# Block 2's RMS norms: token scale taken out of the matmul operand and put into the evictions

## The reference, cut to what matters

```python
def rms_norm_2(x, g):
    y = x * rsqrt(mean(x*x, -1) + EPS)
    return y * g
h = h + hybrid_mixer(rms_norm_2(h, attn_norm_g), w_in, forget_b, ret_norm_g, w_out)   # retention + forgetting attention
h = h + conv_ffn(rms_norm_2(h, ffn_norm_g), w_up, conv_w, conv_b, w_down)             # silu(conv(a)) * b
return rms_norm_2(h, final_norm_g)
```

## Time and profile before

| | |
|---|---|
| median of three runs | 2331.92 us |
| profiled execution, its own time | 2332.22 us |
| its span (first to last instruction) | 2330.3 us |
| granted TensorE clock, mean | 0.994 |
| PE busy | 2264.8 us (97%) |
| DVE / ACT / POOL busy | 908.9 / 886.6 / 1206.2 us |

### The profile page before, as it was taken

The page is one execution under the profiler, slowest core; times in us unless marked ns, Lnnn a source line. Parts: engine busy times, 40 slices in busy tenths (PEclk is TensorE's granted clock), DMA queues, the critical chain, the costliest instruction groups (busy, mean ns, idle before and its releaser), DMA issues.

```text
span 2330.3 us, 31564 instructions
## 1 busy us (share of the span) xinstructions
PE 2264.8 (97%) x12331; PEld 1839.6 (79%) x12331; DVE 908.9 (39%) x1460; ACT 886.6 (38%) x1250; POOL 1206.2 (52%) x1057
## 2 busy tenths in 40 slices
PE   8999999999999999999999999998999999999998
PEld 6777777688888777777768888876888888889896
DVE  5546654422221423666432222245554335313133
ACT  4344342623323443555362332444333224323233
POOL 3666666454444476888654444445213335545452
PEclk9999999999999999999999999999999999999999
DMA  5222222222222232122222223223212112233321
GB/s 155 73 73 73 73 73 73 82 91 93 95 100 90 73 98 64 55 64 64 82 83 90 90 90 108 90 72 103 74 37 54 57 55 73 91 90 106 92 82 64
DMA packets 237945, 188.94 MB, mean 81 GB/s; under 512 B 9279, under 2 KB 228860, under 8 KB 237708
## 3 DMA queue, kind: packets, MB, share of 16 engines
q1 hardware_dynamic: 235726, 183.78, 25.5%
q10 hardware_dynamic: 2110, 3.66, 0.5%
HBM read 185.30 MB, written 2.10 MB: 80 GB/s over the span
## 4 chain that ended last, share of the span: by engine, by line
PE 87%; POOL 5%; ACT 4%; issue 1%; DVE 1%; DMA 1%; ACTq 0%; SPq 0%; DVEq 0%; POOLq 0%
PE ps L2625 43%; PE ps L2856 12%; PE ps L1394 8%; PE ps L638 4%; PE ps L2648 3%; PE ps L2722 3%; PE ps L2658 2%; POOL hdd L423 1%; POOL hdd L421 1%; PE ps L2690 1%; POOL w_lo L1849 1%; PE ps L1477 1%; PE ps L704 1%; POOL a_lo L1864 1%; PE ps L2989 1%
## 5 line engine op out<-in xcount | busy, mean ns | idle before, releaser
L1849 POOL TENSOR_TENSOR w_lo<-raw,w_hi 128x512 fp32r<-128x512 f32 (+2 forms) x756 | 896.5, 1219 | 893.6 <-ACT w_hi L2014 893.0
L2014 ACT ACTIVATE w_hi<-raw 128x2048 fp32r<-128x2048 f32 (+2 forms) x189 | 328.5, 1739 | 577.9 <-PE ps L2625 373.8
L2625 PE MATMUL ps<-b_hi,w_hi 128*128 128x512 f32 x752 | 295.5, 393 | 2.0 <-POOL w_lo L1849 2.0
L2625 PE MATMUL ps<-b_hi,w_lo 128*128 128x512 f32 x752 | 297.4, 396 | 0.0
L2625 PE MATMUL ps<-b_lo,w_hi 128*128 128x512 f32 x752 | 295.7, 393 | 0.0
L2625 PE MATMUL ps<-a_lo,w_hi 128*128 128x512 f32 (+1 forms) x840 | 273.8, 355 | 0.0
L2625 PE MATMUL ps<-a_hi,w_lo 128*128 128x512 f32 (+1 forms) x840 | 273.0, 354 | 0.0
L2625 PE MATMUL ps<-a_hi,w_hi 128*128 128x512 f32 (+1 forms) x840 | 273.0, 354 | 0.0
L2376 DVE TENSOR_TENSOR b_lo<-hv,b_hi 128x512 fp32r<-128x512 f32 x64 | 77.2, 1206 | 284.1 <-ACT b_hi L2101 284.1
L2625 PEld LDWEIGHTS ps<-b_hi,w_hi 128*128 128x128 f32 x752 | 141.3, 188 | 36.4 <-POOL w_lo L1849 2.5
L2625 PEld LDWEIGHTS ps<-a_hi,w_hi 128*128 128x128 f32 x840 | 149.3, 189 | 25.0
(11 more groups left out here) (391 smaller groups left out, 4201.5 us busy)
## 6 DMA issues: line engine op xcount, KB each, us to landing
raw<-in_mlp_w_dram SPq DMA_DIRECT2D x128, 512.0 KB, 4.3
raw<-in_w_up_dram SPq DMA_DIRECT2D x44, 512.0 KB, 5.0
raw<-in_ssd_w_in_dram SPq DMA_DIRECT2D x40, 512.0 KB, 4.8
raw<-in_hgrn_w_in_dram SPq DMA_DIRECT2D x48, 256.0 KB, 3.2
raw<-in_w_in_dram SPq DMA_DIRECT2D x24, 512.0 KB, 4.8
raw<-in_ssd_w_out_dram SPq DMA_DIRECT2D x16, 512.0 KB, 4.2
raw<-in_w_down_dram SPq DMA_DIRECT2D x16, 512.0 KB, 4.0
raw<-in_ple_w_gate_dram SPq DMA_DIRECT2D x12, 512.0 KB, 4.0
```

The lines of the kernel that those rows point to most:

```text
L1849: last = nc.gpsimd.tensor_tensor(w_lo[:, slot, piece], raw[:, slot, i * q:(i + 1) * q], w_hi[:, slot, piece].bitcast(F32), ALU.subtract)
L2014: nc.scalar.activation(w_hi[:, slot, at:at + n], raw[:, slot, 0:n], ACT.Copy).then_inc(whi_ready, 1)
L2625: last = nc.tensor.matmul(ps[:, b + s, 0:nn], w[:, k, m * P:(m + 1) * P], v[:, k, c0 + s * nn:c0 + (s + 1) * nn], start=(k == 0 and first) ...
```

## The change

Both norms (index 0 and 1) of block 2 are taken apart. In place of `xc = res*g*s` and its two parts, ACT makes the high part of `res*g` for each block right behind its square (`scaled_hi`, an Identity with a scale per partition), and DVE the low part (`scaled_lo`); both go to `b_hi` and `b_lo`, and the mixer's and FFN's later operands move from there to `a_hi` and `a_lo`. s is multiplied in by DVE at each eviction: in `projected` from `rs0`, and in the FFN from `lv`, where DVE now takes over the copy of the gate tile from ACT and multiplies the value tile in two instructions. POOL's and DVE's old low parts go. The forget weights `wff` are multiplied by g once; `forget_rows` reads `res`.

The first chunk of `w_in_2` has 24 slices of two pairs: w_hi by b_hi for k below 7 (tile 0, then tile 1), w_lo by b_hi for k below 7, both for k = 7, then w_hi by b_lo. It waits for `w_hi` alone at first. The statistics of both norms run among the products. Chunk 1's cuts come ahead of Ln and Exp in ACT's order. The core of it:

```diff
@@ ACT, per block of the gate stage and of the FFN norm
                 square2(0, k)
+                scaled_hi(0, k)      # b_hi[k] = Identity(res[k], scale = g)
@@ rms2_act
+                if i < 2:
+                    cut_hi(1)
                 sq_at.add(KD)
                 act.wait_ge(sq_used, sq_at())
                 Ln(lv), Exp -> (rs0, lv, pair(6))[i]
-            publish2()
-            cut_hi(1)
+            act.wait_ge(rstd_ready, 5)
             act.dma_start(cb[:], const_b[:, :])
-            act: fp[:, 0, :] = pair(2)
@@ POOL
-            publish2_lo()            # both norms
@@ DVE, gate stage
                     if i and m:
                         add_square(0, m - 1)
+                        scaled_lo(0, m - 1)   # b_lo = res*g - b_hi
+                if i:
+                    scaled_lo(0, KD - 1)
@@ block2_dve
-            rms2_dve(0, C_AN)
-            dve.wait_ge(ff_rows, 1)
             pad_rows(0)
+            dve.wait_ge(ff_rows, 1); dve.wait_ge(rstd_ready, 5)
+            fp[:, 0, :] = pair(0) * rs0
+            pad_rows(1)
             projected(): q, k: tensor_scalar(src) -> scalar_tensor_tensor(src, rs0)
                          others: tensor_scalar(src) -> tensor_tensor(src, rs0)
             projected(); projected()
+            projected()
             maxes(0); maxes(1)
-            projected(); pad_rows(1)
@@ DVE, FFN norm and FFN
-            rms2_dve(1, C_FN)
+            for k in range(KD): scaled_lo(1, k)
+            dve.wait_ge(rstd_ready, 6)
+                    au = pair(gate tile) * lv          # was an ACT copy
                     acc = conv(au)                     # unchanged, three instructions
-                    hv = acc * bank(value tile)
+                    hv = lv * bank(value tile); own.wait(); wait for silu
+                    hv = hv * acc
@@ PE, first chunk of w_in_2
-            pe.wait_ge(free_act, fa()); pe.wait_ge(wlo_ready, chunk(3))
+            pe.wait_ge(free_act, fa(-1)); pe.wait_ge(whi_ready, chunk(1))
+            for m in range(2):
+                if m: pe.wait_ge(free_act, fa())
+                for k in range(KD - 1): wait g_hi[k]; wh x b_hi
+            pe.wait_ge(wlo_ready, chunk(3))
+            for k in range(KD - 1): wl x b_hi, both tiles
+            k = 7: wh, wl x b_hi;  then per tile, per k: wait g_lo[k]; wh x b_lo
                 tile 2: +pe.wait_ge(fl_ready, 1)
@@ PE, order
-            rms2_pe(0)
-            fill(4); forget_rows(); fill(3); forget_sums(); fill(9)
-            pe.wait_ge(s_constb, 16); fill(4); pe.wait_ge(fl_ready, 1)
-            logits(0); logits(1); fill(4); turn_v(0); fill(6); turn_p(0)
+            fill(11); rms2_pe(0); forget_rows(); fill(4); forget_sums(); fill(9)
+            pe.wait_ge(s_constb, 16); fill(8)
+            logits(0); logits(1); fill(3); turn_v(0); fill(3); turn_p(0)
@@ PE, FFN
-            rms2_pe(1)
-            loop of 2: ffn(8)  (high_first on its first chunk);  ffn(6)
+            ffn(8, first=True); ffn(8); ffn(6)
+            # first chunk: wh, wl x b_hi for k = 0..3, rms2_pe(1), k = 4..7, then wh x b_lo
+            # second chunk waits for s (rstd_ready 6) and output tile 39's eviction
```

More of the change, by code:

```diff
@@ L887, in block2_pool @@
             cut_lo(0)
-            publish2_lo()
             def ffn(nt, last):
@@ L906, in block2_pool, with block2_act @@
             ffn(6, True)
-        def block2_act(act, chunk, tile, fa, own, pub, b_at, sq_at, cut_hi, square2):
+        def block2_act(act, chunk, tile, fa, own, pub, b_at, sq_at, cut_hi, square2, scaled_hi):
             def rms2_act(i, before, done=0):
@@ L1176, in projected @@
                             dst = gates[:, j, :]
-                        ins = nc.vector.tensor_scalar(two(dst), src, 1.0, None, ALU.mult)
+                        ins = nc.vector.tensor_tensor(two(dst), src, two(rs0[:]), ALU.mult)
                 else:
@@ L1306, in block2_dve @@
             assert t_at.n == 40 and fd() == FD_FFN, (t_at.n, fd(), FD_FFN)
-            rms2_dve(1, C_FN)
+            add_square(1, KD - 2)
+            for k in range(KD):
+                scaled_lo(1, k)
+            dve.wait_ge(rstd_ready, 6)
             def ffn(nt, base, t0, last=False):
@@ L1337, in ffn @@
                         add_square(2, m - 1)
-            with turns(dve, 2, {tile: 24, fd: 16, own.at: 16, b_at: 8}) as r:
+            with turns(dve, 2, {tile: 24, fd: 16, own.at: 24, b_at: 8}) as r:
                 ffn(8, r * 8, r * 8)
@@ new lines, in products @@
+                def products(m, w, v, k, start=False, stop=False):
+                    for s in range(2):
+                        last = nc.tensor.matmul(ps[:, (6, 4)[m] + s, 0:H2], w[:, k, m * P:(m + 1) * P],
+                                                v[:, k, s * H2:(s + 1) * H2], start=start, stop=stop)
+                    return last
+                for m in range(2):
+                    if m:
+                        pe.wait_ge(free_act, fa())
+                    for k in range(KD - 1):
+                        pe.wait_ge(g_hi, k + 1)
+                        products(m, wh, b_hi, k, start=(k == 0))
+                        if (m + k) % 2:
+                            yield
@@ new lines, in slices @@
+                pe.wait_ge(wlo_ready, chunk(3))
+                for k in range(KD - 1):
+                    for m in range(2):
+                        products(m, wl, b_hi, k)
+                    yield
+                pe.wait_ge(g_hi, KD)
+                for w in (wh, wl):
+                    for m in range(2):
+                        products(m, w, b_hi, KD - 1)
+                    yield
+                for m in range(2):
+                    for k in range(KD):
+                        pe.wait_ge(g_lo, k + 1)
+                        last = products(m, wh, b_lo, k, stop=(k == KD - 1))
+                        if k == KD - 1:
@@ L1648, in squares @@
                 last.then_inc(r_var, 1)
+            fill(11)
+            rms2_pe(0)
+            forget_rows()
             fill(4)
-            forget_rows()
-            fill(3)
             forget_sums()
@@ L2305, in _ @@
             ple_act(squared)
-            block2_act(act, chunk, tile, fa, own, pub, b_at, sq_at, cut_hi, square2)
+            block2_act(act, chunk, tile, fa, own, pub, b_at, sq_at, cut_hi, square2, scaled_hi)
         @block.vector
@@ L2573, in _ @@
             ln_dve(3)
+            dve.wait_ge(s_ff, 32)
+            for k in range(KD):
+                nc.vector.tensor_scalar(wff[:, k, :], wff[:, k, :], col1(C_AN, k), None, ALU.mult).then_inc(ff_pad, 1)
             ple_dve(1, FA_PLE[1])
-            block2_dve(dve, tile, fd, own, pub, b_at, add_square)
+            block2_dve(dve, tile, fd, own, pub, b_at, add_square, scaled_lo)
         @block.tensor
```

226 lines of the change are left out of this document (109 added, 117 removed).

## The result

The kernel after takes 2307.27 us (median of 4 runs, 2306.87 to 2309.24) against 2332.11: ratio 0.9894, interval 0.9881 to 0.9907. The profiled execution took 2309.24 us (span 2307.4).

A forecast was written before the change was run, and what follows sets the result against it. PE, busy 97% of the span, was taken as the bound, with waits and slow clock at two norms. 10.8 + 6.0 − 0.3 = 16.5 us gained gave 2315.4 us on the median of 2331.92; range 2312.5 to 2320.5.

The forecast's parts named there:

- The attention norm: From the gate tiles' end to the fill behind `turn_v`: 11.5 us of waits or slow clock, of which 10.8 are gained.
- The 0.7 kept for `cb` and gaps: Attention norm: part of the 11.5 us expected to remain, 0.2 for `cb` and 0.5 for short semaphore gaps.
- priced at 25.6: PE's work at full clock in the attention norm's 37.1 us, in us, including 2.06 for the statistics.
- The FFN norm: From 1932.61 to 1952.18 us: 19.6 us before, 13.4 at full clock; gain 6.2, taken as 6.0.
- The cost at the last turn: FFN's last up-projection: one more DVE instruction, 0.8 us against 0.57 of room, costs 0.3.
- the walk through the new order: Attention norm, step by step from 1610.42 us: PE goes on without a gap, `logits(0)` near 1633.
- rival D: FFN: DVE's added instructions hold POOL up, PE waits for `w_lo` at 22 chunks; slower, 2353 at 13 us a chunk; chance 0.03.
- A slack of 0.5: Ahead of tile 2: `cb` lands at 1626.8 us, 0.5 before PE wants it; called the tightest point.
- Rival A: Late `cb`, DVE and POOL hold-ups and FFN turns give back 2 to 6 us: 2317.5 to 2321; chance 0.22.
- C: Norms: late `scaled_hi` or low parts keep PE waiting some 3 us each, then slow clock: 2327.5 to 2332; chance 0.03.
- B: Attention steps paced by DVE and ACT eat the earlier start, 6 to 11 us lost: 2321 to 2326; chance 0.07.
- E: More gain than counted: the kept 0.7 and 0.2, an eviction wait or small gaps go too: 2312.5 to 2313.7; chance 0.06.

The follow-up runs named there:

- e1: The kernel before with `small` 88 words a partition smaller, so `a_hi`, `a_lo` and later arrays lie as in the kernel after: 2327.35 us, 0.9979 of before.
- e11: The program of e1 (kernel before, operands placed as in the kernel after) run once more: 2327.29 us, 0.9977 of before.
- e7: The kernel after with DVE multiplying s into the silu's result early, leaving one product behind the value tile: 2308.53 us, 2306.48 us when run again.
- e5: The kernel after, unchanged, run again: 2307.13 us (4 runs).
- e6: The kernel after with the load of `cb` issued behind the forget gate's first ACT instruction: 2314.34 us in one execution.
- e3: The kernel after with PE making the statistics ahead of the first products again at both norms: 2315.81 us.

## Why the prediction was wrong

**The step that failed** is the base of the sum: "Sum. 10.8 + 6.0 − 0.3 = 16.5 us, from the profiled execution's own 2332.22". It takes every stage away from the norms to be as long as before, so it puts the term for the moved operands at nothing. e1 and e11 show that term at 5.0 us, with no instruction changed; 3.05 of it were gained ahead of the first norm. The diff's declarations did show that arrays move, and the trace of before did hold a sign of it: on one and the same line, matmuls that read `a_lo` took 397 ns and those that read `b_lo` 393.

**The attention norm** was right in its mechanism and undersized: 10.8 forecast, 12.9 measured (38.0 less 27.34 − 2.19). Three things make up the difference. The 0.7 kept for `cb` and gaps was not lost. The work was priced at 25.6 and took 25.15, since the statistics take 1.78 and not the 2.06 of the second norm's rows. And 0.9 is the difference between the one profiled norm and the mean of four.

**The FFN norm**: 6.0 forecast; 6.45 measured from before's own profile (19.57 to 13.12), 6.0 from e1 and e11, 6.2 from the mean of the four. **The cost at the last turn**: 0.3 forecast, 0.30 by e7.

By terms, with the norms as e1 and e11 have them, so that nothing is counted twice: 5.0 + 13.3 (38.5 to 25.15) + 6.0 − 0.3 = 24.0, against 24.8 (after) and 25.2 (e5); what is left is inside the interval, about 3 us either way.

**Point by point.** PE goes on into the first chunk at once, and the clock stays at 1.00: right. `logits(0)` came at 1629.95, which is the forecast's 1633 less the 3.05 us that were gained ahead of the norm: the walk through the new order was right as a whole. `w_lo`: POOL's cut took 6.44 us, longer than the 5.92 of the earlier trace rows and under the 6.7 allowed; it ended at 1610.34, before the 14 pairs did. DVE's low part was 0.755 to 1.80 us, the add of two SBUF operands up to 1.67 as in the earlier trace rows, while the FFN's product out of PSUM stayed at 0.675 to 0.690:

```profile
L2342 DVE SCALAR_TENSOR_TENSOR b_lo<-res,pcol,b_hi x16: 755/766/1796, 1582.5 to 1925.2; 128x528 fp32r<-128x528 f32 x16
```

The Trainium skill, page "SBUF — State Buffer", section "Who interferes with whom", says that a DVE instruction with two SBUF inputs contends with a GpSimd instruction that reads SBUF. The trace agrees: a `scaled_lo` of 1.79 us at 1607.40 lies inside POOL's cut of 1603.90 to 1610.34, and the one at 1611.43, with POOL idle, took 0.76. It cost PE nothing, so rival D did not come.

`cb` did come beside chunk 3's load. In this profile it took 7.9 us, in e5's 7.2, so it was hardly slower than the 7.3 of the earlier trace rows; the two loads beside it took 6.9 and 6.4 instead of 4.8:

```profile
cb<-in_const_b_dram ACTq DMA_DIRECT2D x1, 1712.0 KB, 7.9
raw<-in_w_in_dram SPq DMA_DIRECT2D x2, 512.0 KB, 6.9
```

The longer loads agree with the Trainium skill, page "DMA: Bandwidth & Descriptors", section "Issuing engines are not separate DMA queues", by which DMAs that ACT and SP start interleave on the same engines. A slack of 0.5 was forecast; 0.2 was left in this profile and 0.9 in e5's, and e6 shows the price had it run out.

Rival A (waits take back a part) and C did not occur. B did not: the attention steps kept their 5 us of waits and no more. E had the right sign, but its cause, the small terms that I kept, is at most 0.9 of the 8.1 us that were missed.

## What to carry to other kernels

A scale that is one number per row of the output can wait until the eviction, and sums can wait until PE has other work behind it; price both with the slow clock that can follow a wait, which added 1.6 us to one of 3.9 (e6), 2.8 to one of 4.1 (e3) and nothing to one of 1.5 (e3, the FFN norm). When a diff adds, drops or resizes arrays, print the start addresses of both versions before crediting the code: here a fifth of the gain came from 88 words. Take the base from more than one profile of the kernel before.

## What the hardware showed that I had not expected

In the MLP blocks a matmul of 512 columns was 1.7 ns shorter (0.24 us over 144) when its moving operand started on a multiple of 64 bytes than when it started 32 bytes past one, and 2.8 ns in the first chunks (0.09 us over 32), the same in four kernels. Only these two placings were tried, 352 bytes apart, so which property of the address counts stays open; `b_lo`, which lies on a multiple of 64 and never moved, took as long as the placed `a_lo`. And one program, loaded twice, ran at 0.996 and 2308.5 us and then at 0.998 and 2306.5.
